# Expert down weights read in sixteen runs of 88 rows, eight rows of each a block, with the gate-up products written in that row order

## The reference, cut to what matters

```python
def _swiglu(x, wa, wb, wc):
    return (jax.nn.silu(x @ wa) * (x @ wb)) @ wc

    top_v, top_i = lax.top_k(logits, TOP_K)          # TOP_K = 2 of N_EXPERTS = 8
    gates = jax.nn.softmax(top_v, axis=-1)
    ...
    for e in range(N_EXPERTS):
        y = y + comb[:, e:e + 1] * _swiglu(x, we1[e], we3[e], we2[e]).astype(f32)
```

## Time and profile before

| | us |
|---|---|
| median of 3 runs | 2664.95 |
| lowest and highest of them | 2649.84, 2673.07 |
| the profiled execution, its own time | 2646.53 |
| its span, first to last instruction | 2644.8 |
| expert stage, about | 1830 to 2590 |
| TensorE busy over the span | 2300.0 (87%) |
| DMA engines busy in the steady expert loop | 96% |
| HBM read over the span | 456.31 MB |

### The profile page before, as it was taken

How to read it: one execution, slowest core, us unless ns; L and a number is a source line. 1 busy time by engine, 2 the same in 40 slices (tenths; PEclk the granted TensorE clock), 3 DMA queues, 4 the chain that set the end, 5 groups by cost and what they waited for, 6 DMA issues and landing times.

```text
span 2644.8 us, 37813 instructions
## 1 busy us (share of the span) xinstructions
PE 2300.0 (87%) x14297; PEld 1968.9 (74%) x14297; DVE 1534.6 (58%) x2150; ACT 1155.6 (44%) x1553; POOL 185.6 (7%) x257
## 2 busy tenths in 40 slices
PE   6899986778699989998999868587999999999991
PEld 3799753448599989997997535385878878878871
DVE  0466637423543444444566374436888888888884
ACT  3332113332433423323321134315777777777773
POOL 2000101001000000000000011100000100100104
PEclk7699777778799999996998678697999999999995
DMA  7122525271254444540223243305999999999993
GB/s 242 54 80 65 168 58 177 82 230 57 75 165 119 151 128 136 148 141 30 70 74 102 60 145 111 131 12 225 338 378 357 355 383 365 352 381 369 342 353 135
DMA packets 285617, 485.44 MB, mean 184 GB/s; under 512 B 21550, under 2 KB 216632, under 8 KB 285504
## 3 DMA queue, kind: packets, MB, share of 16 engines
q1 hardware_dynamic: 264816, 416.42, 45.6%
q0 software_dynamic: 20688, 67.44, 7.3%
HBM read 456.31 MB, written 26.97 MB: 183 GB/s over the span
## 4 chain that ended last, share of the span: by engine, by line
PE 55%; DVE 6%; DMA 6%; issue 3%; ACT 3%; POOL 0%; ACTq 0%; DVEq 0%; PEldq 0%; PEld 0%; POOLq 0%; SPq 0%
PE banks L850 53%; DMA expert_ring<-in_we 4%; PE banks L854 2%; ACT region_split L1589 1%; DVE region L2109 1%; DVE hidden_t L2109 1%; DVE weights_lower L2109 1%; DVE scratch L2109 1%; ACT hidden_t L1589 1%; DVE expert_lower L2109 1%; ACT scratch L1589 0%; DVE region_split L2109 0%; DVE scratch L2433 0%; DVE weight_ring L2109 0%; DMA hidden_t<-h_rows,pass_tokens 0%
## 5 line engine op out<-in xcount | busy, mean ns | idle before, releaser
L850 PE MATMUL banks<-upper_parts,region_split 128*128 128x320 f32 x1664 | 396.8, 314 | 32.3 <-DVE weights_lower L2109 32.3
L2109 DVE TENSOR_TENSOR expert_lower<-expert_ring,region_split 128x1408 fp32r<-128x1408 f32 (+1 forms) x270 | 388.5, 1467 | 27.4 <-ACT region_split L1589 18.0
L850 PE MATMUL banks<-upper_parts,weights_lower 128*128 128x320 f32 x1248 | 390.1, 313 | 0.0
L850 PE MATMUL banks<-region_split 128*128 128x320 f32 (+1 forms) x1376 | 376.8, 337 | 12.8 <-DVE upper_parts L2109 12.8
L1589 ACT ACTIVATE region_split<-expert_ring 128x1408 fp32r<-128x1408 f32 (+1 forms) x270 | 331.3, 1257 | 62.8 <-DMA expert_ring<-in_we 56.7
L850 PEld LDWEIGHTS banks<-upper_parts,region_split 128*128 128x128 f32 x1664 | 289.7, 192 | 34.5 <-DVE weights_lower L2109 34.5
L850 PE MATMUL banks<-region_split,upper_parts 128*128 128x512 f32 (+1 forms) x996 | 302.6, 380 | 1.6 <-DVE upper_parts L2109 1.6
L850 PE MATMUL banks<-z_weights_upper,upper_parts 128*128 128x256 f32 (+3 forms) x844 | 264.1, 342 | 21.3 <-DVE region_split L2109 21.2
L850 PE MATMUL banks<-expert_lower,upper_parts 128*128 128x512 f32 x720 | 271.3, 377 | 0.0
L850 PEld LDWEIGHTS banks<-region_split 128*128 128x128 f32 x1376 | 245.5, 189 | 28.8 <-issue 13.5
L1589 ACT ACTIVATE region_split<-weight_ring 128x2048 fp32r<-128x2048 f32 (+2 forms) x72 | 141.0, 1960 | 253.0 <-PE banks L850 225.6
(11 more groups left out here) (308 smaller groups left out, 3598.6 us busy)
## 6 DMA issues: line engine op xcount, KB each, us to landing
expert_ring<-in_we SPq DMA_DIRECT2D x240, 704.0 KB, 8.1
expert_ring<-in_we SPq DMA_DIRECT2D x165, 512.0 KB, 4.6
weight_ring<-in_w_ada SPq DMA_DIRECT2D x48, 1024.0 KB, 7.4
weight_ring<-in_w SPq DMA_DIRECT2D x88, 512.0 KB, 4.3
weight_ring<-in_w_in SPq DMA_DIRECT2D x24, 1024.0 KB, 5.3
weight_ring<-in_w SPq DMA_DIRECT2D x16, 1408.0 KB, 6.3
weight_ring<-in_w_out SPq DMA_DIRECT2D x8, 1024.0 KB, 9.7
y_rows<-hidden_t POOLq DMA_DIRECT2D x15, 512.0 KB, 7.6
```

The costliest lines, as they stand in the source:

```text
L850: return nc.tensor.matmul(out, lhsT, rhs, start=first, stop=last)
L2109: return v.tensor_tensor(out, x, y, op)
```

## The change

Two things change. The rows of a down block are chosen otherwise: the 1408 rows of `we2` are cut into 16 runs of 88 rows, and block f takes rows 8 f to 8 f + 7 of each run. Partition 8 i + j then holds row 88 i + 8 f + j. A block is therefore 16 pieces of 32 KB, 352 KB apart in HBM, and the next block takes the next 32 KB of each. The transposes and the down product stay as they are, so DVE has to put hidden unit 88 i + 8 f + j at column 128 f + 8 i + j of `PRODUCT`. It does that as it multiplies, with an output pattern of runs of 8 numbers, in seven pieces where there were three, since a bank's part does not end where a run of 88 ends. Since every transposed block now takes columns from all three parts, TensorE waits for all three before the first transpose.

```diff
+RUN = FE // 16
...
-            by_row = [a[x][l // 2, :, :, :].rearrange("e (k p) n -> e p k n", p=P) for x in ("we1", "we3", "we2")]
+            by_row = [a[x][l // 2, :, :, :].rearrange("e (k p) n -> e p k n", p=P) for x in ("we1", "we3")]
+            down_rows = a["we2"][l // 2, :, :, :].rearrange("e (i f j) n -> e i j f n", i=16, j=8)
...
-                w1, w3, w2 = (x[bass.ds(e, 1), :, :, :].rearrange("e p k n -> p (e k) n") for x in by_row)
-                for src in [w[:, k, :] for k in range(KD) for w in (w1, w3)] if up else [w2[:, f, :] for f in range(NF)]:
+                w1, w3 = (x[bass.ds(e, 1), :, :, :].rearrange("e p k n -> p (e k) n") for x in by_row)
+                w2 = down_rows[bass.ds(e, 1), :, :, :, :].rearrange("e i j f n -> i j (e f) n")
+                for src in [w[:, k, :] for k in range(KD) for w in (w1, w3)] if up else [w2[:, :, f, :] for f in range(NF)]:
...
-                    sp.dma_start(ER[:, place, 0:src.shape[1]], src).then_inc(expert_in[place], 16)
+                    sp.dma_start(ER[:, place, 0:src.shape[-1]], src).then_inc(expert_in[place], 16)
...
                         first, end = PARTS[part]
-                        wait(product_made, n.value("product_made") - 2 + part)
+                        wait(product_made, n.value("product_made"))
                         claim(bank)
...
+                        by_run = PRODUCT.rearrange("p (f i j) -> p i f j", i=16, j=8)
                         for part, (first, end) in enumerate(PARTS):
                             take(silu_made)
                             take(ups_summed)
-                            tt(PRODUCT[:, first:end], SGM[:, first:end], PS[:, 3 + part, 0:end - first], ALU.mult)\
-                                .then_inc(product_made, 1)
+                            at = first
+                            while at < end:
+                                i, rest = divmod(at, RUN)
+                                to = min(end, (i + 1) * RUN) if rest or end - at < RUN else end // RUN * RUN
+                                out = by_run[:, i:max(i + 1, to // RUN), rest // 8:(to - i * RUN) // 8 if rest or to < (i + 1) * RUN else NF, :]
+                                split = lambda x: x.rearrange("p (i f j) -> p i f j", i=out.shape[1], j=8)
+                                ins = tt(out, split(SGM[:, at:to]), split(PS[:, 3 + part, at - first:to - first]), ALU.mult)
+                                at = to
+                            ins.then_inc(product_made, 1)
```

## The result

| | before | after |
|---|---|---|
| median, us | 2668.02 (4 runs, 2649.84 to 2673.07) | 2718.81 (4 runs, 2699.35 to 2725.80) |
| span of the profiled execution, us | 2644.8 | 2714.0 |
| ratio of the times | | 1.0205 [1.0156, 1.0254] |

The change makes the kernel slower: the medians lie 50.8 us apart, and the whole interval of the ratio lies above 1, though not above 1.02. (It is not the quotient of the two medians, which is 1.019.) The time is inside the range of the prediction, because the range took in the milder half of the slow rival; the forecast of 2664, no change, is not where it came out.

A forecast was written before the change was run, and what follows sets the result against it. The expert stage was taken as TensorE's work plus 1.74 us a pass of late DMA engines. 2646.53 + 0 (loads) + 0 (DVE) + 1.5 = 2648 us, 2666 on the scale of medians, set to 2664 for likely packet gains; range 2640 to 2745.

The forecast's parts named there:

- the slow rival: Down-row loads: two engines meet on one path; above 226 ns a packet 1.3 us per ns, up to 2786 us; chance 0.26.
- What bounds the kernel: Expert stage: TensorE's work plus 1.74 us a pass of late DMA engines; they are busy 48.1 of 50.24 us.
- The new source pattern: Down-row loads read as 16 pieces 352 KB apart: no change in packet time, 0 us in the sum.
- the bound: Down-row loads: at best all TensorE waits go, -22.6 us; at worst a packet takes 318 ns.
- The rule that stood right behind it: Trainium skill on DMA loads: the split goes by the outermost dimension of both sides; stated as speaking against the change.
- The signs named for it: Slower reads: DMA share of 1.0 with down rows moving, under 300 GB/s, and ACT waiting in the up phase.
- Each run is shared by two: Down loads still dealt by partitions in groups of four, no engine with its own run; 2664 us, chance 0.2.
- Cleaner reads: Rival, down-row loads: packets go to 159 ns, -13 us to 2651, at most -22.6 to 2642; chance 0.15.
- the 42 ns: Down-row loads before the change: time a packet takes above 159 ns, the rate of the up rows; taken as improvable.
- Seven products: DVE's gate-up products, seven for three: +0.3 to +2.0 us a pass, taken +0.5, hidden, so price 0.
- The wait ahead of the loop: First transposes ahead of the loop wait for all three parts: once +1.5 us, between 0.5 and 3.
- Slower: Whole kernel: outcome slower by over 1% (26.6 us), given 0.25; within 1% had 0.70, faster 0.05.

The follow-up runs named there:

- e4: Kernel before, only the down loads' source changed: 16 pieces of 8 rows, 36 KB apart, some rows read twice; 2713.25 us, ratio 1.0202.
- e10: Kernel before plus 128 probe loads of down rows ahead of the expert stage, eight patterns into various partitions, alone and queued; 3026.33 us, which decides nothing.
- e5: Source and products as in e1, but each down row in two loads of 64 partitions (8 x 8 rows each); 2902.61 us.
- e1: Kernel before with only the change's new source pattern for down loads (16 runs of 88 rows), products and waits as before; 2712.09 us, ratio 1.0202.
- e3: Kernel before with only the down loads' source changed, to 32 runs of 44 rows, four rows each a block; 2658.66 us, ratio 1.0016.
- e7: The whole change, but with 32 runs of 44 rows and products written by runs of 4; against the kernel before 2659.43 us, ratio 1.0018.
- e8: Kernel before with partition p taking row 11 p + f, ordered products, transposes of every eleventh column, wait for all three parts; 2657.22 us, ratio 0.9997.
- e9: Kernel before plus 96 probe loads ahead of the expert stage, six patterns, each eight times alone and eight times queued; 2933.52 us, which decides nothing.
- e2: Kernel before with seven products in the new column order and the wait for all three parts, down loads as before; 2652.91 us, ratio 1.0017.
- e6: Source and products as in e1, but each down row in four loads of 32 partitions (4 x 8 rows each); 3286.85 us.

## Why the prediction was wrong, step by step

**What bounds the kernel: right.** The engines were nearly full, with 226 ns a down packet as the point from which they alone set the pass. At 263 ns they do: the balance gives 53.8 of 54.5 us.

**The new source pattern: the step that failed.** "I take no change, for two reasons": a packet as long as before by the same engine, and the same low bits of the addresses. Both are about HBM and one engine; e4 and e10 show that HBM has no part in it. So the term for the loads stood in the sum at 0, and the runs showed 262 to 263 ns a packet for 189 to 201, and 4.06 us a pass. The path into the on-chip memory was in the bound ("two engines sharing one path at a time", 318 ns) but not in the value. The rule that stood right behind it, that the dealing goes by the outermost dimension, named the mechanism, and I even wrote down what it does here: partitions 8 i to 8 i + 7 for an engine, on two ports shared with another. I left it at "No run here shows it", so it went to a rival and not into the sum.

**The slow rival: right in mechanism, its price a little low.** 1.3 us per ns above 226, at 262 ns: 36 x 1.3 = 47 us, against 50.8 between the medians and some 64 in the traces. In the loop it gives 36 x 88 ns = 3.2 us a pass where 4.06 were measured: it counts the down packets alone, and a pass stays 0.7 us above the balance of the DMA engines even now. The signs named for it came: a share of 1.0 at 256 GB/s with down rows alone. Its size lies between no sharing and full sharing, at 281 ns in a queue alone and 263 in the kernel. That each engine crosses its two paths in turn, so that two engines collide only part of the time, would fit; no run shows the order, and it is not settled why the eight engines of 8 x 8 collide less (203 to 232) than sixteen do, nor why such loads ran at 168 ns inside e5.

**"Each run is shared by two", the change that doesn't do what it says: refuted.** With 16 outermost the time changes, with 32 outermost it doesn't (e1, e3). So the 16 pieces were not dealt in fours; that they went whole, one to an engine, is what fits. 32 x 4 keeps the rate of the old form.

**Cleaner reads: not there.** The down packets' loss against 159 ns in the kernel before is not cured by reading on (e7, e8: 196 to 198 ns in down-only stretches). The queued burst of the old pattern alone runs at 165 to 169 ns, while the same load issued alone had a mean of some 200 ns in e9 and e10. So the 42 ns are not in the source pattern, as I had read them. Nor is it a cost of every packet: in the expert stage of the kernel before the median 4 KB packet takes 159 ns, and the 7% that take over 250 ns make 94% of what the mean lies above that. In the loads of 128 rows that e10 issues alone, the first 16 packets take 385 ns in the mean, the next 16 237, the last 16 159. So the loss fits the starts of loads for which the engines stood idle, as they do for 15% of a down-only stretch; no run changed that in the kernel.

**Seven products: right that they are hidden, the term too large.** 2.00 us for 1.85, +0.15 where I took +0.5. In the groups of DVE by form, the pieces of one pass, and behind them the longer pieces of the kernel before:

```profile
L2112 DVE TENSOR_TENSOR region<-region,banks 128x440 f32<-128x440 f32 x2 | 1.2, 605 | 0.0
L2112 DVE TENSOR_TENSOR region<-region,banks 128x352 f32<-128x352 f32 x1 | 0.5, 515 | 0.0
...
L2112 DVE TENSOR_TENSOR region<-region,banks 128x16 f32<-128x16 f32 x1 | 0.2, 165 | 0.0
```

```profile
L2109 DVE TENSOR_TENSOR region<-region,banks 128x512 f32<-128x512 f32 x30 | 20.6, 688 | 13.7 <-PE banks L850 13.3 <-ACT region L1589 0.3
```

440 columns take 605 ns in runs of 8 and 512 in order take 688, 1.37 and 1.34 ns a column, so the output in runs of 8 costs next to nothing by itself, as the Trainium skill, "Vector Engine (DVE) Microarchitecture Reference", "The SBUF access granule: adjacent pairs", has it; the trace agrees. e2 has the products' price whole: 1.0017 [0.9987, 1.0047].

**The wait ahead of the loop: right.** The timeline of the kernel after (answers to the earlier trace rows):

```profile
1869.88 2.01 DVE L2112 TENSOR_TENSOR region<-region,banks 128x440 f32<-128x440 f32 x7 [0.28 <-ACT region L1592]
...
1871.94 1.32 PE L857 MATMUL banks<-ident,region 128*128 128x128 f32 x8 [0.85 <-DVE region L2112]
...
1874.38 0.48 PE L853 MATMUL banks<-z_weights_upper,upper_parts 128*128 128x512 f32 x1
```

From the start of the products the transposes begin after 2.06 us, before after 0.74: +1.3, where I took +1.5. The second up phase begins after 4.50 us, before after 3.39: +1.1.

**The chances.** Slower had 0.25. The bounds from 159 to 318 ns stood around the one price that mattered, the threshold was 25 ns above the present value, and nothing in the profile held the packets below it. With a rule on the table that said the dealing would change, no change was not the likeliest case.

## What to carry to other kernels

By all that these runs show, a load's source pattern also sets which DMA engine writes which partitions: before its outermost dimension is changed, write down the partitions of each engine, and count the engines that write partitions 32 apart in the same half. Where the DMA engines are nearly full, compute the price per packet from which they bound the stage; if the gap is small, a change in the loads is a risk, whatever it does for the reads. A rate that is below another in a stretch is not a loss to be won before a run of that pattern, alone and in a queue, has shown what belongs to the pattern and what to single issue.

## What the runs showed of the hardware that was not expected

- 16 engines into 64 partitions, in a queue: 322 ns a median packet of 4 KB in partitions 0-63 (e9), 159 ns in 32-95 (e10).
- Packets of the up rows, whose source did not change, took 340 to 380 ns in e5 and e6 with several down packets of the new pattern under way, 220 alone. That they share paths there is not shown apart.
- The distance in HBM between the pieces of a load did not show in the time: 36 KB and 352 KB are alike with 16 pieces (e4, e1), and 176 KB with 32 pieces (e3) and 44 KB with 128 (e8) are like 128 rows in one piece.
- 128 x 4 KB loads that are each waited for have a mean packet of some 200 ns, in a queue 165 to 169 (e9, e10); in e10 it is the first packets of each load that take longer.
- A load of 64 partitions as 8 x 8 uses half of the engines (share 0.50 in e10), one of 32 partitions as 4 x 8 a quarter (0.24 in e9).
